# One order of work on TensorE in a fused attention loop: products with V ahead of all query scores

## What is computed

```python
def fox_block(q, k, v, cq, ck, qpos, kpos):
    s = jnp.einsum('bqhd,bkhd->bhqk', q, k).astype(F32) * (q.shape[-1] ** -0.5)
    s = s + cq.swapaxes(1, 2)[:, :, :, None] - ck.swapaxes(1, 2)[:, :, None, :]
    s = jnp.where(kpos[None, :] <= qpos[:, None], s, -jnp.inf)
    p = jax.nn.softmax(s, axis=-1)
    return jnp.einsum('bhqk,bkhd->bqhd', p.astype(v.dtype), v)
...
    ya = att.reshape(B, L, A_WIDTH) * jax.nn.silu(za)
    y = jnp.concatenate([ya, yb], -1) @ w_out
    return (h + y).astype(h.dtype), (k, v, logf, vn)
```

## Time and profile before

| what | us |
|---|---|
| median of 3 executions | 3817.38 |
| lowest and highest | 3817.26, 3817.94 |
| the profiled execution, its own time | 3815.2 |
| its span in the trace | 3813.2 |
| the steps of the attention loop, in the trace | about 1089 to 2040 |

### The profile page before, as it was taken

The page is one execution under the profiler, slowest core; times in us unless marked ns, Lnnn a source line. Parts: engine busy times, 40 slices in busy tenths (PEclk is TensorE's granted clock), DMA queues, the critical chain, the costliest instruction groups (busy, mean ns, idle before and its releaser), DMA issues. The chain is left out here.

```text
span 3813.2 us, 43864 instructions
## 1 busy us (share of the span) xinstructions
PE 3346.2 (88%) x14087; PEld 1804.3 (47%) x14087; DVE 2207.8 (58%) x3145; ACT 752.4 (20%) x1448; POOL 120.7 (3%) x221
## 2 busy tenths in 40 slices
PE   2999999999268989989999499999999999757799
PEld 1444444444133333333333276776767767512343
DVE  1777888888448878988998034443443444313211
ACT  1011111110122121222131022232233222103111
POOL 0000000000010000000000000000000000000000
PEclk8999999999679999999999799999999999877899
DMA  5566666665145646635556500000000000234232
GB/s 209 171 194 192 194 205 196 195 203 178 67 146 156 196 126 181 185 116 176 173 146 206 201 12 11 11 22 11 14 19 11 22 11 11 23 76 153 96 110 73
DMA packets 243046, 447.99 MB, mean 117 GB/s; under 512 B 38529, under 2 KB 69249, under 8 KB 241850
## 3 DMA queue, kind: packets, MB, share of 16 engines
q1 hardware_dynamic: 222602, 412.12, 35.8%
q0 software_dynamic: 5696, 18.88, 1.4%
q10 hardware_dynamic: 14592, 15.24, 1.2%
HBM read 390.16 MB, written 55.99 MB: 117 GB/s over the span
## 5 line engine op out<-in xcount | busy, mean ns | idle before, releaser
L523 PE MATMUL ep_PJ<-ep_w,ep_xT 128*128 128x512 f32 x1792 | 782.5, 596 | 10.4 <-ACT ep_xT L383 10.4
L523 PEld LDWEIGHTS ep_PJ<-ep_w,ep_xT 128*128 128x128 f32 x1792 | 337.9, 191 | 420.5 <-issue 414.1
L1683 PE MATMUL mb_B<-ml_w,mp_xT 128*128 128x512 f32 x1024 | 446.4, 594 | 0.0
L444 DVE TENSOR_TENSOR ep_kpage<-ep_kpage,ep_q_bc 128x1024 f32<-128x1024 f32 x256 | 311.6, 1217 | 130.8 <-DMA ep_kpage<-in_cache_k_dram 130.6
L452 DVE TENSOR_REDUCE g_scores<-ep_kpage 128x1024 f32 (+1 forms) x256 | 311.7, 1218 | 11.5 <-DVE ep_kpage L444 3.3
L1053 DVE TENSOR_TENSOR at_vpage<-at_vpage,g_scores 128x1024 f32<-128x1024 f32 x248 | 302.0, 1218 | 18.1 <-DMA at_vpage<-in_cache_v_dram 18.1
L975 ACT ACTIVATE at_PT<-at_S,g_negc 128x512 f32<-128x512 f32 (+3 forms) x320 | 181.9, 619 | 628.9 <-PE at_S L1150 628.9
L1683 PEld LDWEIGHTS mb_B<-ml_w,mp_xT 128*128 128x128 f32 x1024 | 192.1, 190 | 230.1 <-issue 229.5
L1056 DVE TENSOR_TENSOR at_acc<-at_acc,at_vpage 128x1024 f32<-128x1024 f32 x240 | 294.0, 1225 | 8.2
L1696 PE MATMUL mb_B<-mp_xT,ml_w 128*128 128x128 f32 x2048 | 254.6, 291 | 0.0
L1696 PEld LDWEIGHTS mb_B<-mp_xT,ml_w 128*128 128x128 f32 x2048 | 252.1, 207 | 0.0
(11 more groups left out here) (443 smaller groups left out, 3597.6 us busy)
## 6 DMA issues: line engine op xcount, KB each, us to landing
ep_kpage<-in_cache_k_dram SPq DMA_DIRECT2D x512, 256.0 KB, 3.0
at_vpage<-in_cache_v_dram SPq DMA_DIRECT2D x512, 256.0 KB, 3.0
ep_w<-in_even_w_in_dram SPq DMA_DIRECT2D x8, 1796.0 KB, 30.8
ml_w<-in_odd_w_in_dram SPq DMA_DIRECT2D x24, 512.0 KB
ep_x<-in_x_prompt_dram SPq DMA_DIRECT2D x16, 512.0 KB
scratch_mix<-ep_mixed SPq DMA_DIRECT2D x16, 512.0 KB, 3.0
at_stage<-scratch_mix SPq DMA_DIRECT2D x32, 256.0 KB, 3.8
at_xh<-in_x_prompt_dram POOLq DMA_DIRECT2D x32, 256.0 KB, 3.9
```

The costliest lines, as they stand in the source:

```text
L444: nc.vector.tensor_tensor(kpage[i][:], kpage[i][:], q_bc[r][:].unsqueeze(1).to_broadcast([P, 2, AW]), ALU.mult).then_inc(pr[i], 1)
L523: op = nc.tensor.matmul(BANK[name][:], xT[r][:, k, :], w[:, k, COL[name]:COL[name] + 512], start=k == 0, stop=k == KC - 1)
L1683: op = nc.tensor.matmul(B[banks[m]][:], xT[:, k, :], w[:, k, col + 512 * m:col + 512 * m + 512], start=k == 0, stop=k == KC - 1)
```

## The change

In each step TensorE takes `product(i-1)` before any block of `score_queries`, and VectorE takes `gate` before any maximum. Nothing is added or removed, and no buffer, plan table or transfer is changed.

```diff
@@ VectorE, attend
             for i in range(STEPS + TAIL):
                 if i < STEPS:
                     todo = list(range(p1_end[i - 1] if i else first[1], p1_end[i]))
-                    for n in todo[:1]:
-                        maximum(n)
                     if i and i == first[unit_of[i]]:
                         gate(unit_of[i] - 1)
-                    for n in todo[1:]:
+                    for n in todo:
                         maximum(n)
@@ TensorE, attend
                 score_keys(i)
                 todo = list(range(p1_end[i - 1] if i else first[1], p1_end[i]))
-                for n in todo[:1]:
-                    score_queries(n)
                 here = list(range(t_end[i], t_end[i + 1]))
                 for e in here:
                     if turns[e][0] != "m":
...
                 if i:
                     product(i - 1)
-                for n in todo[1:]:
+                for n in todo:
                     score_queries(n)
```

## The result

| what | us |
|---|---|
| before, median of 4 executions on the same chip | 3817.3 (3814.9 to 3817.9) |
| after, median of 4 | 4033.2 (4026.9 to 4038.0) |
| after by before | 1.0569, 95% interval 1.0556 to 1.0582 |
| the profiled execution of after, and its span | 4032.05, 4030.0 |

A forecast was written before the change was run, and what follows sets the result against it. The prediction took TensorE to bound the loop, with VectorE only 54 us behind. Its terms, 63 + 47 + 28 + 9 + 6 - 6 + 45 = 192 us on 3815.2, gave 4007 (4009 against the median), range 3925 to 4055.

The forecast's parts named there:

- (a): Projections in one of the next two steps after a projection wait for VectorE's residual: nine places, 63 us.
- (b): With no projection in the next two steps, a later query block waits for the maximum behind VectorE's burst: 47 us.
- (c): A projection near a unit's end: the burst delays `gate` or the "m" turn, 28 us.
- (d): At 14 unit starts, one wait of 4.7 us replaces 4.0 us: 0.65 us each, 9 us in all.
- (e): Ten steps with two query blocks in units 3, 7, 11: second waits 1.4 us for its predecessor's maximum; 6 us net.
- (f): A gain at step 107: the late "d" turn and page load no longer idle TensorE, 6.3 us taken off.
- The sign on VectorE: Sign expected in the changed profile: VectorE's idle time ahead of maxima grows by 7 us for each of 24 projections.
- (g): Lower granted clock behind new TensorE waits over 3 us: 18 waits at 2.5 us each, 45 us.
- weaker coupling: Rival, chance 0.18: residual waits mostly absent because bursts overlap what waits anyway; 122 us slower, 3937 us.
- The clock stays down: Rival, chance 0.11: in units 4 and 5 the clock doesn't return between waits; 40 us or so more, 4049 us.
- Nothing: Rival, chance 0.03: VectorE's slack lies where the bursts now fall, so both even out; 3817 us within a few.
- faster: Rival, chance 0.06: the earlier gate at 14 unit starts decides, 26 us less, 3791 us.

The follow-up runs named there:

- the matched pairs: Changed kernel with VectorE taking the residual first, plus each projection's page pairs planned one step earlier: 3879.3 us, ratio 1.0172.
- The unit starts: Changed kernel with VectorE's old order at unit starts (first maximum, gate, other maxima), TensorE's order still changed: 4004.8 us, ratio 1.0496.
- the last kernel: Changed kernel with 9, 9 and 7 useless matmuls ahead of the three projections that wait longest for a residual: 4021.7 us, ratio 1.0540.

## Why the prediction was right, and what it missed

Point by point, by its own steps:

- *(a), residual waits, 63 us*: measured 63.1, in nine entries, at the nine places: 9.80, 5.98, 9.38, 6.04, 7.99, 5.97, 6.04, 6.33 and 5.62 us, against 9.9, 5.9, 9.0, 6.1, 8.0, 5.9, 6.1, 6.2 and 6.0. That these waits are a cost of their own is shown by the kernel with the residual first.
- *(b), maxima behind a burst, 47 us*: the ten waits are 4.91, 1.86, 2.32, 5.50, 4.88, 1.08, 5.36, 5.36, 5.50 and 6.61, in sum 43.4. Short by 1.7 each are the ones at 61 and 106. The second is not a query block's: the "d" turn of step 63 waits for VectorE's last page addition.
- *(c), units' ends, 28 us*: the two `gate` places have one wait of 12.22 us each, which is the 4.7 of (d) and 7.5; the two long "m" turns 6.25 and 6.26 (5.8 predicted).
- *(d)*: 4.62 us at a full unit start (4.7 predicted). Over the 14 starts, without the 7.5 us of (c), the waits grew by 8 us (9 predicted).
- *(e)* was too small: 1.35 us at seven of the ten steps (1.4 predicted), but 2.49, 2.99 and 3.05 at the others, and in all 12 us more than before instead of 6.
- (b) to (e) and (f) in sum: maxima and "m" turns were to grow by 47 + 28 + 9 + 6 - 6 = 84 us; they grew by 70.2 + 14.8 = 85.0. That this is so close is partly luck: the query blocks of (b) gave 5.5 us less and (e) 6 more.
- *(f)*: the wait of 11.41 us for a page load is gone, and TensorE waits 1.08 us for a maximum at that place instead of 6.27. The group of page multiplications idles 2.3 us in all, 18.1 before.
- *The sign on VectorE*: its idle time ahead of maxima was to grow by 7 us for each of 24 projections, 168 us; it grew by 204.6 (127.9 to 332.5).
- *(g), the clock, 45 us*: measured 52.3 us of longer busy time. After has 36 waits over 3 us in the loop and before 16, so 20 more and not 18; two of the 20 are waits for staged blocks, which the prediction didn't have. Spread over the 20, that is 2.6 per wait. The Trainium skill (TensorE: Matmul & The Clock Gate, "What's actually happening") says "the ramp penalty is <1% of a typical kernel span" of the cold matmuls at a kernel's start. The prediction took it as a cap on everything that the clock can cost, and as such it does not hold for this kernel: 52.3 of 4030.0 us is 1.3%, for the growth alone.

**The step that failed** is the sentence "In a step without a projection this shifts nothing". For the query block and what VectorE does behind it that is true. But the turns stay where they were in the program while the query block and the product changed places with them: a turn now stands right behind `score_keys`, with no query block ahead of it. Against VectorE, which sets when page loads can start, it is earlier by a query block and a product, an estimated 1.17 + 1.87 = 3.0 us. The loads that the turns wait for stand in SP's queue behind those page loads. Cost: 16.7 us of waits, two of them over 3 us (3.51 and 3.26) and followed by the lower clock. The kernel with queries last only at projections shows it from the other side (7.7 us, no more than before), the one with the longer look-ahead removes it (19 us). The prediction had said that SP's order stays, and had not asked what a transfer in it is late for. The sentence had put this term at nothing. With the 7 us of clock it makes up 24 of the 25 us between 4007 and the profiled 4032.

The rivals: *weaker coupling* fell with nine full waits for residuals. *The clock stays down* fell: the three projections with the longest waits take 5.55, 6.60 and 5.30 us for their first half and the second half 3.60 each time, so the clock came back within the projection. *Nothing* and *faster* fell with the time. With the bursts at the right place the same order on TensorE is no faster than the old one (3801 and 3802, both with the longer look-ahead); only mixed with it, and with VectorE's new plan, it gives 3785.

The experiments were predicted less well than the change. The remaining loss with queries first at projections (3887, expected up to 3850) and the matched pairs (3879, expected up to 3855) missed mostly by the same term as the prediction: 15 and 29 us of staged blocks that no expectation had; in the first, 18 us of clock came on top. The unit starts (28 us gained, 57 at first expected) missed by 13 us of staged blocks and by the clock, of which 8 us came back instead of 35. Only 8 waits over 3 us were gone from the loop (28 left of 36) where 14 had been counted, and each gave back 1 us and not 2.5.

What stays open: the 14 us of the look-ahead in the kernel before, of which only 7 are seen as waits in one execution; at which length a wait brings the clock down; and whether the old order, with VectorE's plan changed in the same way, would reach 3785 too.

## What to carry to other kernels

- When two engines that work in fixed order meet at single buffers, the place of the handing-over instruction matters more than the amount of work. Moving the query block behind the projection in 24 of 160 steps, with nothing added, cost 4.8% (the whole change 5.7%): the partner's burst of up to 12.7 us was planned for the old place. Move the plan along with the order (3801 with a longer look-ahead, 3802 for the kernel before with the same), or leave both.
- Such a loss can be summed beforehand: take from the timeline the start-to-start times of each piece, count how much of the engine's own work lies between the new place of the signal and the next place that needs the answer, and subtract. Here nine waits came out within 0.4 us each.
- For each instruction that moves, and for each that another moves past, ask also for the transfers it waits for, and what stands ahead of them in their queue, even if that queue's order is not touched.
- Look at the length of waits and not only at their sum. The fastest kernel here waits nearly as long as the old order with the same look-ahead, but in shorter pieces, and TensorE is busy 17.5 us less.

## What the runs showed of the hardware

- Waits of a few us cost more than they last. With 20 more waits over 3 us in the loop TensorE was busy 52.3 us longer at the same work, 2.6 us each, in stretches at 1.2 instead of 2.4 GHz. Over all kernels here its busy time follows the number of such waits: 3328.6 us with 3, 3346.2 with 16, 3381.6 with 27, 3398.5 with 36, about 2.1 us for each; single kernels lie up to some 10 us off that line. Filling three of them with 22.2 us of useless matmuls made the kernel 11.5 us faster.
- The same length of wait does not always do it: behind 4.62 us the query block of 128 columns took 0.80 us at 1161.17 and 0.49 at 1194.26 and 1293.25 in after, and behind a wait of 2.07 us in the last kernel a projection was slow, while behind 3.05 us in the kernel with queries first at projections a query block was not (1.13 us at 1721.30).
- An f32 matmul of 512 columns stands in the trace as two rows of 0.43 us at full clock (18 rows took 7.89 us in the last kernel); whoever fills or counts by rows must halve.
